# A two-block transformer kernel: the second layer's first norm in the last expert value steps, position tables from skewed rows, and the down projection's first halves in the gate loop

## The chip, the cores and the metric

One program runs on one core of a Trainium2 chip. The metric is the device time of one execution in microseconds (us). Engines: PE is TensorE (PEld its weight loads), DVE is VectorE, ACT is ScalarE, POOL is GpSimd, SP is SyncE, which issues the DMAs.

## The reference, cut to what matters

The program is one forward pass in float32 over 256 tokens and 256 context tokens, 1024 channels, in two blocks of two layers each. A layer of the first block is

```python
h = _modulate(_rmsnorm(x, norm1_g[l]), mod[0], mod[1])     # h * (1 + scale) + shift
p = h @ w_in[l]                                            # then four mixers, merged and added to x
h = _modulate(_rmsnorm(x, norm2_g[l]), mod[3], mod[4])
x = x + mod[5] * _peer(h, *peer_args)                      # 16384 experts, 16 of them for each of 8 heads
```

Context rows go through the same with their own modulation. `_peer` scores every expert against every token, and sums value rows with weights. A layer of the second block mixes (layer 0 a gated delta rule, layer 1 sparse attention with a relative position bias taken from `rel_bias`; both attend to a memory too), and then adds a gated feed-forward part:

```python
gate, val = jnp.split(h @ w_up, 2, axis=-1)
gate = causal_dwconv(gate, conv_w) + conv_b
return (jax.nn.silu(gate) * val) @ w_down                  # w_down is 2816 x 1024
```

## The kernel before, in words

Most products are made of three matmuls: each operand is split into a high half (ACT copies it to a rounded type) and a low half (DVE or POOL subtracts the high half), and high x high, high x low and low x high are summed in PSUM (`products_of`, L106). The program is a row of stages (`stage`, L53). Within a stage the engines run their own lists of instructions and meet by semaphores; at its end all of them wait for each other. K.ps is the eight PSUM banks of 128 x 512.

*Expert values.* `peer` (L1821) ends with U = 64 value steps for layer 0 (indices `m`; the DMA table of the page counts those of both layers as 128). Step m fetches 256 value rows (1 MB, `pr_w`), the kept scores (`pr_gs`) and the chosen weights (`pr_g`). DVE multiplies scores and weights (`multiply`, L2366), ACT and DVE split both operands (L2221, L2383 to L2394), and TensorE adds 6 products into each of 8 banks, two banks for each of four tiles of 128 tokens (`combine`, L2111): 48 matmuls a step. Step m's two operands must be split before it starts. SP waits for TensorE's step m before it refills that step's slot (L1945). After the last step, DVE adds the eight banks, times the modulation, to the rows x (L2396 to L2403).

*The second layer's first norm.* `first_norm` (L2507) is a stage of its own, and it calls `norm` (L499). SP fetches two small tables, a 480 KB table and the masks (`PositionsBeside`, L3594), four rows of modulation, the gain row and the first two weight tiles of the next projection. ACT squares four tiles of rows and takes the root; DVE makes (1 + scale) times gain, scales each tile and adds the shift; TensorE turns 32 blocks of 128 x 128; ACT copies the high halves, DVE subtracts for the low ones. Beside this TensorE makes the position tables: one product of 32 x 384 that is stored with a skew in DRAM (`po_rows`, for layer 1's bias), and 60 small ones for the bias of the compressed attention (`cmp_bias`). The next stage, `branch_inputs` (L2406), starts with the projection.

*Attention to memory.* `attend` (L3026) works through items: a score, its scaling and maximum on DVE, the exponential on ACT, two transposes, a copy on ACT, a product with the values and a scaling. Three items are under way at once. Layer 0 of the second block has 8 items. Before them SP fetches two tiles of the next projection's weights, 1.5 MB each; ACT splits the first behind the last item. `compressed_attention` (L3469) is the first stage of layer 1's attention.

*Feed-forward part.* `conv_glu` (L3688) runs J = 22 gate steps: TensorE makes gate and value columns, ACT copies the gate, DVE convolves, ACT takes silu, DVE multiplies and both split the result. SP fetches the first four tiles of `w_down` near the end. The next stage, `down` (L3798), splits a tile of `w_down` at each step k (ACT L3826, DVE L3853), and TensorE adds it into four banks in 12 matmuls; SP refills a slot when its low half is done, and at k = 8 it also fetches the gain row and, in layer 0, three 1 MB tiles of the next layer's projection, one behind the other. Its first matmul waits for the first low half.

## Time and profile before

| | |
|---|---|
| median of 3 runs | 4334.24 us (4333.1 to 4334.87) |
| profiled execution, its own time | 4332.16 us |
| span of the profile | 4330.4 us |
| mean granted clock of TensorE | 0.971 |
| PE / DVE / ACT / POOL busy | 94% / 62% / 43% / 10% of the span |
| DMA | 833 MB, 192 GB/s, q1 busy 57.4% of 16 engines |

Times in the rows are microseconds from the span's start. A timeline row gives start, duration, engine, line, operation, output<-inputs, shapes and count; in brackets stands how long the engine was idle before it and what ended that. Several operations of a kind in a row are merged (x8). A row of groups gives busy us and mean ns of one. The granted clock is 1.00 at 2.4 GHz and 0.50 at 1.2 GHz.

### The profile page before, as it was taken

What the parts mean: (1) busy time and instruction counts of PE and PEld (TensorE: products, weight loads), DVE (VectorE), ACT (ScalarE), POOL (GpSimd) and SP (SyncE); (2) the same over time, 40 slices, a digit from 0 to 9 for tenths busy, and PEclk for the clock granted to TensorE, in tenths of its full rate; (3) what the DMA queues carried; (4) which work ended last, traced back from release to release, by engine and by line L of the source; (5) the groups of instructions that cost most, each with busy time, mean ns of one, the idle gap of its engine ahead of it and who ended that gap; (6) DMA issues with size and microseconds to landing.
All of it is one profiled execution on the core that took longest, in us unless ns stands there. A gap on an engine that the chain in (4) does not pass through costs nothing. (4 is left out here: it accounts for less than half of the span.)

```text
span 4330.4 us, 62619 instructions
## 1 busy us (share of the span) xinstructions
PE 4084.7 (94%) x25222; PEld 3567.3 (82%) x25222; DVE 2704.3 (62%) x5412; ACT 1840.5 (43%) x2400; POOL 413.2 (10%) x118
## 2 busy tenths in 40 slices
PE   7999899999999999999989899999998988998898
PEld 5876788788877888888788799998886887988697
DVE  5736668899941455555575588754666664653665
ACT  3433233477743322222245445544444444543453
POOL 2222034200000000000004240000000012000000
PEclk8999999999999999999899999999999999999999
DMA  6431224377788777777544456777886522554354
GB/s 241 142 101 61 94 88 140 123 285 296 293 314 289 240 242 243 243 243 243 185 134 140 147 174 194 256 287 268 290 283 224 163 71 78 157 186 140 93 163 144
DMA packets 523642, 833.18 MB, mean 192 GB/s; under 512 B 20829, under 2 KB 398877, under 8 KB 502073
## 3 DMA queue, kind: packets, MB, share of 16 engines
q1 hardware_dynamic: 523354, 829.18, 57.4%
q8 instruction: 200, 3.28, 0.3%
q14 instruction: 88, 0.72, 0.1%
HBM read 692.19 MB, written 136.92 MB: 191 GB/s over the span
## 5 line engine op out<-in xcount | busy, mean ns | idle before, releaser
L113 PE MATMUL bank<-hThi_l,pr_whi 128*128 128x512 f32 (+1 forms) x2304 | 786.9, 342 | 16.6 <-DVE pr_wlo L2269 6.7
L113 PE MATMUL bank<-hTlo_l,pr_whi 128*128 128x512 f32 (+1 forms) x2304 | 779.1, 338 | 0.0
L113 PE MATMUL bank<-hThi_l,pr_wlo 128*128 128x512 f32 (+1 forms) x2304 | 777.6, 338 | 0.0
L113 PE MATMUL bank<-pr_whi,pr_ahi 128*128 128x512 f32 x1536 | 600.0, 391 | 9.7 <-DVE pr_alo L2393 9.7
L113 PE MATMUL bank<-pr_wlo,pr_ahi 128*128 128x512 f32 x1536 | 599.0, 390 | 0.0
L113 PE MATMUL bank<-pr_whi,pr_alo 128*128 128x512 f32 x1536 | 598.7, 390 | 0.0
L2151 ACT ACTIVATE pr_whi<-pr_w 128x2048 fp32r<-128x2048 f32 x270 | 517.2, 1915 | 126.7 <-DMA pr_w<-peer_v_in 124.0
L113 PEld LDWEIGHTS bank<-hThi_l,pr_whi 128*128 128x128 f32 x2304 | 441.1, 191 | 66.1 <-POOL pr_wlo L2026 8.1
L113 PEld LDWEIGHTS bank<-hThi_l,pr_wlo 128*128 128x128 f32 x2304 | 440.8, 191 | 46.1
L113 PEld LDWEIGHTS bank<-hTlo_l,pr_whi 128*128 128x128 f32 x2304 | 441.4, 192 | 42.2
L2269 DVE TENSOR_TENSOR pr_wlo<-pr_w,pr_whi 128x2048 fp32r<-128x2048 f32 x102 | 233.4, 2289 | 269.0 <-ACT pr_whi L2151 268.9
L113 PEld LDWEIGHTS bank<-pr_whi,pr_ahi 128*128 128x128 f32 x1536 | 289.0, 188 | 73.6 <-DVE pr_wlo L2386 11.1
L2221 ACT ACTIVATE pr_ahi<-pr_a 128x1024 fp32r<-128x1024 f32 (+1 forms) x128 | 108.5, 847 | 563.8 <-DVE pr_a L2377 364.5
L113 PEld LDWEIGHTS bank<-pr_whi,pr_alo 128*128 128x128 f32 x1536 | 289.2, 188 | 60.3
L113 PEld LDWEIGHTS bank<-pr_wlo,pr_ahi 128*128 128x128 f32 x1536 | 289.2, 188 | 59.6
L2165 ACT ACTIVATE pr_s<-bank 128x512 f32<-128x512 f32 (+1 forms) x256 | 125.2, 491 | 471.3 <-PE bank L113 454.2
L2386 DVE TENSOR_TENSOR pr_wlo<-pr_w,pr_whi 128x2048 fp32r<-128x2048 f32 x128 | 292.4, 2284 | 21.1 <-ACT pr_whi L2151 21.1
L1290 POOL TENSOR_TENSOR gr_wlo<-gr_w,gr_whi 128x2048 fp32r<-128x2048 f32 x30 | 137.4, 4580 | 1709.3 <-ACT gr_whi L1495 1709.3
L2375 DVE TENSOR_TENSOR pr_a<-pr_g 128x512 f32<-128x512 f32 x128 | 82.8, 689 | 307.9 <-DMA pr_g<-dense_weights 307.9
L2026 POOL TENSOR_TENSOR pr_wlo<-pr_w,pr_whi 128x2048 fp32r<-128x2048 f32 x40 | 188.3, 4708 | 379.0 <-ACT pr_whi L2151 379.0
L113 PE MATMUL bank<-gu_Thi,gu_whi 128*128 128x256 f32 x704 | 200.2, 284 | 3.5 <-PEq L61 3.5
L113 PE MATMUL bank<-hThi_l,gr_whi 128*128 128x512 f32 (+1 forms) x512 | 184.1, 360 | 17.0 <-ACT mx_gate L1578 7.3
(609 smaller groups left out, 8241.5 us busy)
## 6 DMA issues: line engine op xcount, KB each, us to landing
pr_w<-peer_u_in SPq DMA_DIRECT2D x128, 1024.0 KB, 5.7
pr_w<-peer_v_in SPq DMA_DIRECT2D x128, 1024.0 KB, 5.0
dense_weights<-pr_buf SPq DMA_DIRECT2D x20, 4096.0 KB, 16.4
pr_g<-dense_weights SPq DMA_DIRECT2D x64, 1024.0 KB, 9.1
gu_w<-ffn_w_up_in SPq DMA_DIRECT2D x88, 512.0 KB, 5.2
gr_w<-w_in_in SPq DMA_DIRECT2D x32, 1024.0 KB, 5.3
expert_scores<-pr_s SPq DMA_DIRECT2D x64, 512.0 KB, 7.1
pr_gs<-expert_scores SPq DMA_DIRECT2D x64, 512.0 KB, 5.9
```

What stands on the lines that cost most here:

```text
L113: ins = pe.matmul(psum, a, b, start=first and i == 0, stop=last and i == len(terms) - 1)
L1290: pool.tensor_tensor(w_lo[:, held.slot(n), :, :], wt[:, held.slot(n), :, :], w_hi[:, n % slots, :, :].bitcast(F32), ALU.subtract).then_inc ...
L2026: pool.tensor_tensor(w_lo[:, n % ring, :, :], wt[:, n % ring, :, :], w_hi[:, s, :, :].bitcast(F32), ALU.subtract).then_inc(lo_ready, 1)
L2151: act.activation(w_hi[:, n % slots, :, :], wt[:, n % ring, :, :], ACT.Copy).then_inc(hi_ready, 1)
L2165: act.activation(act_s[:, m % 3, j, :], K.ps[i % 4][:, 0:tw], ACT.Gelu_apprx_tanh).then_inc(freed, 1)
L2221: act.activation(a2[0][:, m % aslots, :, :], a[:, m % aslots, :, :], ACT.Copy).then_inc(a_hi, 1)
L2269: dve.tensor_tensor(w_lo[:, n % ring, :, :], wt[:, n % ring, :, :], w_hi[:, n % slots, :, :].bitcast(F32), ALU.subtract).then_inc(lo_later, 1)
L2375: last = dve.tensor_tensor(sums[:, :, e, :], both_halves[:, :, e, 0, :], both_halves[:, :, e, 1, :], ALU.add)
L2386: dve.tensor_tensor(w_lo[:, n % ring, :, :], wt[:, n % ring, :, :], w_hi[:, n % slots, :, :].bitcast(F32), ALU.subtract).then_inc(v_lo, 1)
```

## The change

Three things, in one edit.

1. The stage `first_norm` is gone. A class NextNorm is called from layer 0's `peer`. The last two value steps go by tiles of tokens: for each tile, both steps, then the next tile. When a tile's two banks are done, DVE adds them to x, ACT squares the tile and takes its root (a root per tile in place of one), DVE scales it in two halves, TensorE turns it (two tiles later), ACT copies the high half with the shift as a bias, and DVE makes the low half from the bank, the shift and the high half. The shift is now a column of 8 numbers per partition, and the copies and low halves are 128 wide (32 of each in place of 8 that were 512 wide). The scaled rows lie in slots of the value ring that are free by then. SP fetches modulation and gain at steps 10, 16 and 22, and the two weight tiles of the projection after the last multiply. (1 + scale) times gain is made at step 32 (`m == U // 2`).
2. The position tables' one product moves to the attention to memory of the second block's layer 0 (class Positions): the widening stands behind the first item's maximum on DVE, the product ahead of the first transposes on TensorE, the copy behind the first exponential on ACT, the store behind the weight tiles on SP. The 60 small products are gone: the compressed attention adds the masks to elements of the skewed bias instead (three small operations on DVE, ahead of the bias operation L3566).
3. In the last gate step ACT and DVE make both halves of the first two tiles of `w_down`; `down` starts with k = 2 on these engines, its slots are shifted by one, SP starts two fetches earlier without a wait, and the three next tiles are fetched at k = 9, 12 and 15.

`hT` and the projection's ring are allocated once for both layers.

```diff
+        if after:
+            spare = (first_v + U - 3) % 3
+            row_pairs = [wt[:, spare, :, :].rearrange("p (e j) c -> p e (j c)", e=2), held.wide[:, spare, :, :].rearrange("p (e j) c -> p e (j c)", e=2)]
+            after.hold(mem, lambda t: row_pairs[t // 2][:, t % 2, :])
...
+                    if after and m in (10, 16, 22):
+                        after.fetch(sp, (m - 10) // 6)
                 sp.wait_ge(mod_in, 32)
+                if after:
+                    sp.wait_ge(mulled, U)
+                    after.fetch_tiles(sp)
+                    after.land(sp)
...
+                for m in range(U - 2 if after else U):
+                    combine(m, range(outs))
+                for t in range(tiles if after else 0):
+                    for m in (U - 2, U - 1):
+                        combine(m, range(2 * t, 2 * t + 2), False)
+                    if t >= 2:
+                        after.turn(pe, t - 2)
+                for t in range(2 if after else 0):
+                    after.turn(pe, tiles - 2 + t)
...
+                for t in range(tiles if after else 0):
+                    if t >= 3:
+                        after.round_row(act, t - 3)
+                    after.square(act, t)
+                    after.root(act, t)
+                    if t == 0:
+                        after.first_hi(act)
+                for t in range(3 if after else 0):
+                    after.round_row(act, tiles - 3 + t)
...
+                    if after and m == U // 2:
+                        after.prepare(dve)
...
+                for t in range(tiles):
+                    if after and t:
+                        after.shift_square(dve, t - 1)
+                    add_out(2 * t)
+                    if after and t == 1:
+                        dve.wait_ge(used, U - 2)
+                    if after and t:
+                        after.scale_row(dve, t - 1)
+                    add_out(2 * t + 1)
+                    if after and t == 1:
+                        after.first_lo(dve)
+                if after:
+                    after.rest_of_row(dve, 0)
+                    after.shift_square(dve, tiles - 1)
+                    after.rest_of_row(dve, 1)
+                    after.scale_row(dve, tiles - 1)
+                    for t in range(2, tiles):
+                        after.rest_of_row(dve, t)
...
+class NextNorm:
...
+    def bank(self, g):
+        return self.K.ps[(6 + g) % 8][:, :].rearrange("f (n p) -> f n p", n=4)
+
+    def fetch(self, sp, i):
+        K, l = self.K, self.l
+        if i < 2:
+            sp.dma_start(self.scale[:, i, :], K.ada[l, i:i + 1, D:2 * D].broadcast_to([P, D])).then_inc(self.mods_in, 16)
+            sp.dma_start(self.shift[:, i, :], K.ada[l, i, 0:D].rearrange("(k p) -> p k", p=P), allow_slow_non_contiguous=True).then_inc(self.mods_in, 16)
+        else:
+            sp.dma_start(self.gain[:, :], K.dram["norm1_g"][l:l + 1, :].broadcast_to([P, D])).then_inc(self.mods_in, 16)
...
+    def prepare(self, dve):
+        dve.wait_ge(self.mods_in, 80)
+        for s in range(2):
+            dve.scalar_tensor_tensor(out=self.scale[:, s, :], in0=self.scale[:, s, :], scalar=1.0, in1=self.gain[:, :], op0=ALU.add, op1=ALU.mult).then_inc(self.step, 1)
+
+    def square(self, act, t):
+        if t:
+            act.wait_ge(self.squared, t)
+        act.wait_ge(self.done, 2 * t + 2)
+        act.activation(self.K.junk[:, 0:D], self.x[:, t, :], ACT.Square, scale=D ** -0.5, accum_out=self.ss[:, t:t + 1]).then_inc(self.squared, 1)
+
+    def root(self, act, t):
+        act.wait_ge(self.shifted, t + 1)
+        act.activation(self.ss[:, t:t + 1], self.ss[:, t:t + 1], ACT.Sqrt).then_inc(self.rooted, 1)
...
+    def scale_row(self, dve, t):
+        at = self.ss[:, t:t + 1]
+        dve.wait_ge(self.rooted, t + 1)
+        dve.reciprocal(at, at).then_inc(self.step, 1)
+        dve.wait_ge(self.step, t + 3)
+        for c in range(2):
+            part = slice(c * 512, (c + 1) * 512)
+            dve.scalar_tensor_tensor(out=self.h(t)[:, part], in0=self.x[:, t, part], scalar=at, in1=self.scale[:, t // 2, part],
+                                     op0=ALU.mult, op1=ALU.mult).then_inc(self.scaled, 1)
+
+    def turn(self, pe, t):
+        for g in range(2 * t, 2 * t + 2):
+            pe.wait_ge(self.scaled, g + 1)
+            for j in range(4):
+                k = 4 * (g % 2) + j
+                last = pe.transpose(self.bank(g)[:, j, :], self.h(t)[:, k * P:(k + 1) * P], self.K.ident[:, :])
+            last.then_inc(self.turned, 1)
+
+    def round_row(self, act, t):
+        for g in range(2 * t, 2 * t + 2):
+            at = self.place(g)
+            act.wait_ge(self.turned, g + 1)
+            for j in range(4):
+                k = at[0].start + j
+                last = act.activation(self.hT[0][:, k, at[1]], self.bank(g)[:, j, :], ACT.Identity, bias=self.shift[:, t // 2, k:k + 1])
+            last.then_inc(self.hi_done, 1)
+
+    def rest_of_row(self, dve, t):
+        for g in range(2 * t, 2 * t + 2):
+            at = self.place(g)
+            dve.wait_ge(self.hi_done, g + 1)
+            for j in range(4):
+                k = at[0].start + j
+                last = dve.scalar_tensor_tensor(out=self.hT[1][:, k, at[1]], in0=self.bank(g)[:, j, :], scalar=self.shift[:, t // 2, k:k + 1],
+                                                in1=self.hT[0][:, k, at[1]].bitcast(F32), op0=ALU.add, op1=ALU.subtract)
+            last.then_inc(self.lo_done, 1)
...
+class Positions:
...
+    def widen(self, dve):
+        dve.wait_ge(self.arrived, 32)
+        dve.tensor_copy(self.many[:, :, :], self.rel[:, :, None].broadcast_to([32, GH, P // GH])).then_inc(self.wide, 1)
+
+    def product(self, pe):
         pe.wait_ge(self.wide, 1)
+        pe.matmul(self.K.ps[7][:, 0:3 * P], self.many[:, :, :].rearrange("b h r -> b (h r)"), self.hot[:, :], start=True, stop=True).then_inc(self.spread, 1)
+
+    def take(self, act):
+        act.wait_ge(self.spread, 1)
+        act.activation(self.rows[:, :], self.K.ps[7][:, 0:3 * P], ACT.Copy).then_inc(self.rows_out, 1)
...
                 score(1)
+                if positions:
+                    positions.product(pe)
...
                 exponential(0)
+                if positions:
+                    positions.take(act)
...
                 maximum(0)
+                if positions:
+                    positions.widen(dve)
...
+                for t in range(2):
+                    seen = N_CMP if t else (P - 32) // 16 + 1
+                    at = 1 + (1 - t) * P // 16
+                    chain(dve.tensor_tensor(cmp_bias[:, t, :, 0:seen], bias[:, :, :].rearrange("p h (n i) -> p h n i", i=16)[:, :, at:at + seen, 15],
+                                      cm[:, 0, t, 0:seen][:, None, :].broadcast_to([P, GH, seen]), ALU.add))
+                    if seen < N_CMP:
+                        dve.tensor_copy(cmp_bias[:, t, :, seen:N_CMP], cm[:, 0, t, seen:N_CMP][:, None, :].broadcast_to([P, GH, N_CMP - seen]))
...
+                else:
+                    act.wait_ge(down_first, 32)
+                    for k in range(2):
+                        act.activation(buffers.down[0][:, k + 1, :], dn_w[:, k, :], ACT.Copy).then_inc(down_hi, 1)
...
+                if i == J - 1:
+                    for k in range(2):
+                        dve.wait_ge(down_hi, k + 1)
+                        dve.tensor_tensor(buffers.down[1][:, k + 1, :], dn_w[:, k, :], buffers.down[0][:, k + 1, :].bitcast(F32), ALU.subtract)
...
-                sp.wait_ge(lo_ready, k - 3)
+                if k >= 6:
+                    sp.wait_ge(lo_ready, k - 5)
                 sp.dma_start(w[:, k % 4, :], K.dram["ffn_w_down"][l][k * P:(k + 1) * P, :]).then_inc(loaded[k % 4], 16)
                 if k == 8:
                     sp.dma_start(behind.gain, behind.source).then_inc(gain_in, 16)
-                    if ahead:
-                        ahead.fetch(sp, first_in, rest_in)
+                if ahead and k in (9, 12, 15):
+                    ahead.fetch_tile(sp, (k - 9) // 3, first_in, rest_in)
...
-            for k in range(J):
+            for k in range(2, J):
...
-                act.activation(halves[0][:, k % 3, :], w[:, k % 4, :], ACT.Copy).then_inc(hi_ready, 1)
+                act.activation(halves[0][:, (k + 1) % 3, :], w[:, k % 4, :], ACT.Copy).then_inc(hi_ready, 1)
...
-                pe.wait_ge(lo_ready, k + 1)
+                if k >= 2:
+                    pe.wait_ge(lo_ready, k - 1)
...
```

## Rows read from the trace of the kernel before

**Rows 1.** Windows: five engines busy us (instructions), granted clock, DMA share, GB/s

```profile
1500.00:1600.00 100.00, 100.00 (x443) 82.84 (x442) 52.71 (x45) 26.72 (x18) 0.00 (x0) 1.00 0.80 252
...
2170.00:2175.00 5.00, 4.12 (x19) 4.15 (x20) 1.42 (x7) 1.91 (x1) 0.00 (x0) 0.50 0.23 36
```

**Rows 2.** Timeline of PE: start, duration, operation [idle before, releaser]

```profile
2134.20 0.39 PE L113 MATMUL bank<-pr_whi,pr_alo 128*128 128x512 f32 x1
...
2142.64 1.61 PE L3626 MATMUL bank<-po_hot,po_many 32*128 32x384 f32 x2 [8.06 <-DVE po_many L3635]
...
2144.05 12.80 PE L3630 MATMUL bank<-po_rel,po_chot 32*128 32x8 f32 x60
...
2170.88 0.55 PE L113 MATMUL bank<-hThi_l,wpair 128*128 128x256 f32 x1 [6.61 <-PEq L61]
```

**Rows 3.** Timeline of DVE around the old norm

```profile
2116.52 1.22 DVE L2393 TENSOR_TENSOR pr_alo<-pr_a,pr_ahi 128x1024 fp32r<-128x1024 f32 x1
...
2125.17 0.69 DVE L2400 TENSOR_TENSOR pr_tmp<-bank,pr_mod 128x512 f32<-128x512 f32 x1 [7.43 <-PE bank L113]
...
2126.51 0.69 DVE L2400 TENSOR_TENSOR pr_tmp<-bank,pr_mod 128x512 f32<-128x512 f32 x1
...
2149.76 2.36 DVE L2517 SCALAR_TENSOR_TENSOR mod_l<-mod_l,gain_l 128x1024 f32<-128x1024 f32 x2 [4.90 <-DMA gain_l<-norm_g_in]
...
2165.62 4.87 DVE L572 TENSOR_TENSOR hTlo_l<-bank,hThi_l 128x512 fp32r<-128x512 f32 x8
```

**Rows 4.** Timelines of ACT, DVE and PE at the end of layer 0's gate loop

```profile
3828.50 0.51 ACT L3735 ACTIVATE gu_cv<-gu_cv,gu_cb 128x256 f32<-128x256 f32 x1 [1.22 <-DVE gu_cv L3790]
...
3835.46 2.95 ACT L3826 ACTIVATE dn_hi<-gu_down_w 128x1024 fp32r<-128x1024 f32 x3 [0.81 <-PEq L61]
...
3831.25 0.35 DVE L3788 TENSOR_SCALAR gu_cv<-gu_gp,gu_cw 128x256 f32<-128x256 f32 x1 [1.45 <-ACT gu_gp L3749]
...
3834.67 0.42 DVE L3773 TENSOR_TENSOR gu_actlo<-gu_bs,gu_acthi 128x256 fp32r<-128x256 f32 x1
...
3837.82 0.50 PE L113 MATMUL bank<-dn_hi,gu_acthi 128*128 128x512 f32 x1 [4.15 <-DVE dn_lo L3853]
```

**Rows 5.** Waits in 3812 to 3910: who for whom, us, times, longest

```profile
ACT dn_hi L3826 <- DMA gu_down_w<-ffn_w_down_in: 7.4, 3, 7.0
...
PE bank L113 <- DVE dn_lo L3853: 6.3, 2, 4.2
```

**Rows 6.** Groups by form: busy us, mean ns | idle before

```profile
L3141 DVE SCALAR_TENSOR_TENSOR b_cat<-bank,at_weight,b_cat 128x128 f32<-128x128 f32 x32 | 11.2, 351 | 8.2 <-PE bank L3075 7.6
...
L642 DVE SCALAR_TENSOR_TENSOR xrows<-xrows,small,dn_gain 128x512 f32<-128x512 f32 x4 | 2.7, 746 | 0.0
...
L3106 ACT ACTIVATE at_pt<-bank 128x128 f32<-128x128 f32 x16 | 4.1, 256 | 0.0
...
L3095 ACT ACTIVATE at_pr<-at_sc,at_max 128x128 f32<-128x128 f32 x16 | 6.4, 401 | 3.5 <-DVE at_max L3128 3.4
```

**Rows 7.** Timeline of ACT in the old norm

```profile
2136.39 1.06 ACT L533 ACTIVATE junk<-xrows 128x1024 f32<-128x1024 f32 x1 [20.89 <-PEq L61]
...
2141.10 1.28 ACT L535 ACT_TABLE_LOAD   x1
```

**Rows 8.** Groups of 1500 to 2100, the expert value loop of layer 0

```profile
L2375 DVE TENSOR_TENSOR pr_a<-pr_g 128x512 f32<-128x512 f32 x110 | 71.1, 689 | 273.4 <-DMA pr_g<-dense_weights 273.4
```

**Rows 9.** DMA issues of 2170 to 2174: KB, median us to landing

```profile
bi_wb<-cv_dw_b_in SPq DMA_DIRECT2D x1, 1.0 KB, 1.8
```

**Rows 10.** DMA issues of 2136 to 2170

```profile
po_hot<-bucket_rev_in SPq DMA_DIRECT2D x1, 48.0 KB, 2.2
```

**Rows 11.** Timeline of PE in layer 0's attention to memory

```profile
3640.69 0.69 PE L3066 MATMUL bank<-ident,at_pr 128*128 128x128 f32 x2 [0.75 <-ACT at_pr L3095]
```

**Rows 12.** Timeline of DVE in the compressed attention

```profile
3995.22 0.19 DVE L3568 COPY nc_kcT<-bank 128x30 f32<-128x30 f32 x1 [7.84 <-PE bank L3522]
```

**Rows 13.** Windows by stretch, the start of layer 0's down projection

```profile
3838.00:3843.00 5.00, 5.00 (x16) 3.91 (x17) 2.04 (x2) 0.94 (x2) 0.00 (x0) 0.66 0.78 238
```

More of the change, by code:

```diff
@@ L462, in fetch, with fetch_tile @@
                 sp.dma_start(dst, src).then_inc(rest if i else first, 16)
+    def fetch_tile(self, sp, i, first, rest):
+        for dst, src in self.tiles[i]:
+            sp.dma_start(dst, src).then_inc(rest if i else first, 16)
     def land(self, sp, first, rest):
@@ L496, in ahead, with norm @@
         return Ahead(tiles, self.halves[0][:, 0, :, 0:cw], self.halves[1][:, 0, :, 0:cw], self.wt[:, 0, :, 0:cw])
-def norm(K, rows, tiles, gain_of, shift_of, out, chans=None, loads=(), prepare=None, ahead=None, beside=None):
+def norm(K, rows, tiles, gain_of, shift_of, out, chans=None, loads=(), ahead=None):
     n = len(tiles)
@@ L503, in norm @@
     groups = [(i, c) for i in range(n) for c in range(0, KD, 4)] if chans is not None else []
-    with stage(K, "squared", "eps_added", "rooted", "step", "scaled", "turned", "hi_done", "lo_done", "loads_in", "first_in", "rest_in", "ahead_hi",
-               *(beside.names if beside else ())) as \
-            (block, squared, eps_added, rooted, step, scaled, turned, hi_done, lo_done, loads_in, first_in, rest_in, ahead_hi, *others):
-        if beside:
-            beside.use(*others)
+    with stage(K, "squared", "eps_added", "rooted", "step", "scaled", "turned", "hi_done", "lo_done", "loads_in", "first_in", "rest_in", "ahead_hi") as \
+            (block, squared, eps_added, rooted, step, scaled, turned, hi_done, lo_done, loads_in, first_in, rest_in, ahead_hi):
         def bank(g):
@@ L1814, in __init__ @@
         self.lo = mem.enter_context(K.nc.sbuf_tensor(f"pr_wlo{l}", [P, ring, KD, 256], F32R))
+        with K.nc.sbuf_tensor(f"pr_wide{l}", [P, self.slots, KD, 256], F32) as wide:
+            self.wide = wide
         self.hi = mem.enter_context(K.nc.sbuf_tensor(f"pr_whi{l}", [P, self.slots, KD, 256], F32R))
@@ L2119, in combine @@
                     pe.wait_ge(a_lo, m + 1)
-                    for o in range(outs):
+                    for o in wanted:
                         t, c = divmod(o, 2)
@@ L2523, in first_layer, with branch_ring @@
+def branch_ring(K, l):
+    with ExitStack() as upper:
+        upper.enter_context(K.nc.sbuf_tensor(f"ring_hole_l{l}", [P, 67 * 256], F32))
+        ring = Ring(K, upper, KD, MIX + 16, 2)
+        side = ModulationBeside(K, l, upper) if l == 0 else None
+    return ring, side, ring.ahead(K.dram["w_in"][l], [(CV_OFF, MIX), (CV_OFF + MIX, MIX)])
+def first_layer(K, l, x, s_cols, hT, hT_wide, rings):
     nc = K.nc
@@ L3023, in _, with attend @@
                 close(1, a, four(o[:, 1], a))
-def attend(K, items, scale, ahead):
+def attend(K, items, scale, ahead, positions=None):
     nc = K.nc
@@ L3625, in tensor @@
+    def product(self, pe):
         pe.wait_ge(self.wide, 1)
-        pe.matmul(K.ps[6][:, 0:3 * P], self.many[:, :, :].rearrange("b h r -> b (h r)"), self.hot[:, :], start=True, stop=True).then_inc(self.spread, 1)
-        for t in range(2):
-            for n in range(N_CMP):
-                c = (t * N_CMP + n) * GH
-                last = pe.matmul(K.ps[7][:, c:c + GH], self.chot[:, t, n, :], self.rel[:, :], start=True, stop=True)
-        last.then_inc(self.spread, 1)
-    def first(self, dve):
-        dve.wait_ge(self.arrived, 64)
-        dve.tensor_copy(self.many[:, :, :], self.rel[:, :, None].broadcast_to([32, GH, P // GH])).then_inc(self.wide, 1)
-        dve.wait_ge(self.spread, 1)
-        dve.tensor_copy(self.rows[:, :], self.K.ps[6][:, 0:3 * P]).then_inc(self.rows_out, 1)
@@ L3935, in build @@
         s_cols = K.s_cols = sb("s_cols", [P, KD, 2])
-        cmp_bias = sb("cmp_bias", [P, 2, GH, N_CMP])
-        for l in range(DEPTH):
-            first_layer(K, l, x, s_cols, cmp_bias)
+        with ExitStack() as first:
+            hT_hi = first.enter_context(nc.sbuf_tensor("hThi", [P, KD, TALL], F32R))
+            with nc.sbuf_tensor("hTwide", [P, KD, TALL], F32) as hT_wide:
+                pass
+            hT = hT_hi, first.enter_context(nc.sbuf_tensor("hTlo", [P, KD, TALL], F32R))
+            rings = [branch_ring(K, l) for l in range(DEPTH)]
+            for l in range(DEPTH):
+                first_layer(K, l, x, s_cols, hT, hT_wide, rings)
         x2 = x[:, 2:4, :]
         K.tri, K.mem = sb("tri", [P, P]), mem
-        second_block(K, x, cmp_bias)
+        second_block(K, x)
 def buckets(dist):
```

185 lines of the change are left out of this document (86 added, 99 removed).

## The prediction

> **What bounds the kernel now.** I read the page first: TensorE is busy 94% of the span, so time is lost only where TensorE stands still or works on something small. The windows by stretch then show one large hole, between the expert values of layer 0 and the first projection of layer 1. When TensorE comes out of it, the granted clock is 0.50, the lower of its two levels (1.2 GHz), for the first 5 us of the projection [rows 1]. TensorE's own order of time gives its edges: the last value matmul starts at 2134.20 (0.39 long), the first projection matmul at 2170.88 [rows 2]. That is 36.3 us in which TensorE does 60 tiny table products (12.8 us) and 32 transposes. The same view of VectorE shows why the hole lasts: its norm waits for the gain row until 2149.76 and its last low half ends at 2165.62 + 4.87 = 2170.49; 0.39 us later the next stage begins [rows 2, 3]. Two further holes are at the end of the gate loops (TensorE starts the down projection at 3837.82 after 4.15 us idle, and likewise in the other layer) and one is inside layer 0's down projection (6.3 - 4.15 = 2.15 us, behind a 7.0 us wait for weights) [rows 4, 5].
>
> **Part 1, the norm: what bounds it after the change.** I take the trace's times and lay the new order over them. A value matmul starts every 0.227 us (443 of them fill 100 us [rows 1]; 48 a step: the two last steps run from 2112.8 to 2134.6). Now rows of tokens go one after the other, each with 24 matmuls, 5.44 us.
> - TensorE, row 0: twelve matmuls of step 62 until 2115.5. Then step 63, the last, is wanted, whose low half ends at 2116.52 + 1.22 = 2117.74 [rows 3]; before, it was wanted only at 2123.7. A new stall of 2.2 us. Rows 0 to 3 then end at 2120.5, 2126.0, 2131.4 and, with 8 transposes between (0.9 us), 2137.8.
> - VectorE: adding half a row takes 1.34 us (two starts of L2400 [rows 3]), so 2.7 a row. Scaling a row is two 512-wide operations of 0.746 [rows 6], 1.4 + 0.2 for the reciprocal. The first low half of the projection's weights, moved as it is, takes 2.3. The new low halves are 128 wide with a pointer, as L3141, 0.351 us each [rows 6]; back to back they overlap by some 0.07, so 8 take 2.2 us, against 1.2 for the two 512-wide ones that they replace.
> - ScalarE: a square is 1.06 + 0.19 us, the root's table is loaded once, 1.28 [rows 7]. The high halves are 128-wide copies, now with a bias from a pointer. The plain copy is 0.256, the 128-wide exponential with a bias pointer 0.401 [rows 6]. I take 0.39, 0.30 back to back, 2.4 us a row: it is nearest to the form that has the pointer.
> - Laid end to end: row 0 is added by 2122.1 and squared by 2123.3; root 2124.8 (table). Row 1 is added by 2129.2, the weights' low half done 2131.4. Row 2 added by 2135.9, its root 2137.6. Row 3 added by 2141.7, squared 2142.9. VectorE meanwhile makes row 0's low half, 2141.7 to 2143.8, and adds eps to row 3 (2143.9); root 2144.1. ScalarE can round row 1 only after that root, to 2146.6; VectorE's low half of row 1 ends 2147.7, row 3 is scaled by 2149.4, row 2's low half ends 2151.5, row 3's 2153.7. With 0.39 for the stage and half a microsecond for the chance that the clock falls in the new stall, the projection starts at 2154.6 instead of 2170.9: **16.3 us gained**.
> - Bounds: with the plain copy's 0.256 and low halves at the 0.28 of a plain 128-wide operation, 13 such on the path, the end is near 2151.5 (19 us gained). With every semaphore hop of some 0.25 us missed at a dozen handovers, and the clock falling in the new stall (1.7 us on TensorE), it is near 2158 (13 us).
>
> The Trainium skill, page "ScalarE: Activation LUTs", section "What ACT_TABLE_LOAD costs", gives a pointer operand some 93 ns more per ACTIVATE, here against the change: 32 copies with a pointer in place of 8 wide ones. The traced 0.401 with a pointer against 0.256 without agrees in sign. By that page's 280 + 0.833 x 128 = 387 ns my end stands; without its rule it would be some 1 us earlier.
>
> What is moved in front costs nothing as I read it. In the value loop VectorE waits 273.4 us over 55 steps for the weighted choices, 5.0 a step [rows 8], and another 6.0 us lie between its last low half and TensorE's need. So the two 1.2 us scale operations at step 32 vanish, and so do two 512 KB rows, two column loads and one gain row on SP's queue at steps 10, 16 and 22: if a column load holds the queue 4 us (1024 packets of 4 bytes; 256 such landed in 1.8 us [rows 9]), the next weights land 4 us later and are still in time. If that cover were gone, each would cost its own length. The weights of the projection (2 MB) are fetched after the last multiply, 2114.4, and have 10 us until ScalarE wants the first. The projection itself starts at half clock as before: nothing gained.
>
> **Part 2, tables from skewed rows.** The 60 products and the table's arithmetic go with the old stage, counted above. The product that spreads the rows comes back in layer 0's attention to memory, and there it is on the path. The two loads start with the stage (3637.9), the second lands 2.2 us after its issue [rows 10], 3640.5; VectorE widens to 3640.7; TensorE's product is 1.61 us [rows 2], to 3642.35, and the first transposes, which stood at 3640.69 [rows 11], come 1.7 us late. ScalarE's copy of 384 columns (0.5) stands ahead of the second exponential: 2.1 late. All eight items follow, and so does the end of the stage: **2.0 us lost**. Bounds: 0.5 if later items catch up, 3.5 if the 1.5 MB store, behind 3 MB of output weights, ends the stage. The three small operations in the compressed attention stand ahead of 7.84 us in which VectorE waits for TensorE [rows 12]: nothing, and at most 1.0 if that cover were gone.
>
> **Part 3, down projection.** Two copies (2 x 1.06) go ahead of ScalarE's silu at 3828.50, of which 1.2 us were idle: silu 0.9 late. Two low halves (2 x 1.22) go on VectorE ahead of the last convolution, which stood at 3831.25: they run 3830.3 to 3832.7, after them a 0.4 low half, so it starts at 3833.0. Of the 1.75 us, 0.5 is absorbed, since the last product waited for TensorE anyway: the stage ends 1.2 later than 3834.67 + 0.42 = 3835.1. In return the down stage's first matmul no longer waits for 1.06 + 1.22: TensorE starts 0.4 after the stage does, 3836.7, not 3837.82 [rows 4]. Gain 1.1, twice: 2.2. The clock fell in the gap of 4.15 us (0.66 over the 5 us behind it [rows 13]) and I expect it to fall in one of 3.1 us as well; bounds 0 and 5.5 for both layers, the upper if neither falls. In layer 0 the three 1 MB tiles no longer go into the queue together: each takes some 2.8 us of it, and a weight has 4.6 us of slack at 2.8 us a step. The stall of 2.15 us [rows 5] goes; bounds 1 and 2.5. **4.3 us gained**.
>
> **Sum.** 16.3 - 2.0 + 4.3 = 18.6 us off the profiled 4332.16 is 4313.6. The median of the runs is 2.1 us above the profiled run, so I forecast 4334.24 - 18.6 = **4315.6 us**. Part 1 alone moves every later stage against the clock's changes; that moves single microseconds either way.
>
> **Rivals.**
> - The tail is bound by handovers between three engines, not by VectorE's sum, and the two other parts bring nothing: 13 - 3.5 + 1 = 10.5 gained, 4323.7. For: row 3 passes through eight handovers. Against: in my schedule VectorE hardly idles after 2124. 12%.
> - The clock is kept in the gaps before the down projections, and the tail is at its lower bound: 19 - 1.5 + 6.5 = 24, 4310. Against: the gaps shrink by a quarter only, and the clock fell in the old ones [rows 13]. 10%.
> - ScalarE's tables: if square, root and identity did not share a set, each of four rows would load twice, 8 x 1.28 = 10 us, 5 to 8 of it on the path: 4322. Against: after the one load of the old root and in the down stage, squares and root follow with one load (here [rows 7]). 5%.
> - The change doesn't do what it says: the new stall becomes the bound because fetches of steps 62 and 63 come later. They are issued as before, so 3%, 4326.
> - The slower side: the column loads starve TensorE. They stand on SP's queue ahead of the next weighted choices. With 5.0 + 6.0 us of slack, of which I trust 6, it takes over 15 us a load for two of them to eat 18.6 us; at 25 us each, 2 x 19 - 18.6 = 19 slower, 4354. For: 4-byte packets, 1024 a load. Against: 256 of them took 1.8 us. 5%.
>
> **How the numbers follow.** Forecast 65%, the rivals as above. A measurement of this kernel can tell 0.2%, 8.7 us, from no change. Faster by more than that: the forecast, the first rival mostly, the second and third: 0.90. Within: 0.05. Slower: 0.05. Range: the bounds of the three parts, not all at one end, and so that both first rivals are inside: 4309 to 4324.
>
> **What would show it.** Right: a stall of about 2.2 us on TensorE before the second half of row 0; the first projection matmul some 20 us after the last value matmul would have ended (2154 to 2156); one table load there; VectorE busy over 90% from 2131 on; 2 us more between first and second transposes in layer 0's attention; no wait for weights in layer 0's down projection. Wrong: any TensorE gap in the value loop at steps 10 to 23, or more than one table load in the tail.

## The result, and the profile after

| | before | after |
|---|---|---|
| median of the runs beside each other | 4333.67 us | 4298.1 us |
| ratio after to before, 95% interval | | 0.9929, 0.9916 to 0.9943 |
| the same comparison, repeated with 5 runs and 16 | 4327.73 us | 4297.15 us, 0.9934, 0.9921 to 0.9948 |
| profiled execution, its own time | 4332.16 us | 4297.31 us |
| span, mean granted clock | 4330.4 us, 0.971 | 4295.5 us, 0.972 |
| PE / DVE / ACT / POOL busy | 94 / 62 / 43 / 10% | 95 / 63 / 43 / 10% |

By the ratios the change gains 29 to 31 us (0.0066 and 0.0071 of 4330); the medians lie 30.6 and 35.6 us apart. I had forecast 18.6 and a range that ended at 4309: the kernel is faster than that.

First the timeline of TensorE around the norm, then of ScalarE and VectorE there.

```profile
2116.14 0.48 PE L113 MATMUL bank<-pr_whi,pr_ahi 128*128 128x512 f32 x1 [2.33 <-DVE pr_alo L2407]
...
2139.89 0.66 PE L2630 MATMUL bank<-ident,pr_wide 128*128 128x128 f32 x4
2147.66 1.97 PE L2630 MATMUL bank<-ident,pr_wide 128*128 128x128 f32 x8 [7.11 <-DVE pr_wide L2622]
2152.80 0.55 PE L113 MATMUL bank<-hThi,wpair 128*128 128x256 f32 x1 [3.17 <-PEq L61]
```
```profile
2123.37 1.28 ACT L2602 ACT_TABLE_LOAD   x1
...
2137.25 2.17 ACT L2639 ACTIVATE hThi<-bank,nn_shift 128x128 fp32r<-128x128 f32 x8
...
2141.08 2.15 DVE L2648 SCALAR_TENSOR_TENSOR hTlo<-bank,nn_shift,hThi 128x128 fp32r<-128x128 f32 x8
...
2144.59 2.16 DVE L2648 SCALAR_TENSOR_TENSOR hTlo<-bank,nn_shift,hThi 128x128 fp32r<-128x128 f32 x8 [1.30 <-ACT hThi L2639]
```

The new stall is there (2.33 us, foretold 2.2), one table load, and the projection starts at 2152.80. The after trace runs 1.74 us ahead before the changed place, so [rows 2]'s 2170.88 stands for 2169.14: 16.3 us gained.

The start of either down projection (TensorE, layer 0 and 1), and three of ScalarE's copies in layer 1, first after, then before. These copies wait for TensorE, so their distance is the length of one step of 12 matmuls.

```profile
3816.56 1.19 PE L113 MATMUL bank<-dn_pair,gu_acthi 128*128 128x512 f32 x2 [2.56 <-PEq L61]
...
4226.89 0.70 PE L113 MATMUL bank<-dn_pair,gu_acthi 128*128 128x512 f32 x2 [2.57 <-PEq L61]
...
4238.13 1.06 ACT L3974 ACTIVATE dn_pair<-gu_down_w 128x1024 fp32r<-128x1024 f32 x1 [1.66 <-PE bank L113]
4240.85 1.06 ACT L3974 ACTIVATE dn_pair<-gu_down_w 128x1024 fp32r<-128x1024 f32 x1 [1.66 <-PE bank L113]
4243.57 1.06 ACT L3974 ACTIVATE dn_pair<-gu_down_w 128x1024 fp32r<-128x1024 f32 x1 [1.66 <-PE bank L113]
```
```profile
4258.42 0.80 PE L113 MATMUL bank<-dn_hi,gu_acthi 128*128 128x512 f32 x1 [4.15 <-DVE dn_lo L3853]
...
4271.54 1.06 ACT L3826 ACTIVATE dn_hi<-gu_down_w 128x1024 fp32r<-128x1024 f32 x1 [1.73 <-PE bank L113]
4274.34 1.06 ACT L3826 ACTIVATE dn_hi<-gu_down_w 128x1024 fp32r<-128x1024 f32 x1 [1.74 <-PE bank L113]
4277.14 1.06 ACT L3826 ACTIVATE dn_hi<-gu_down_w 128x1024 fp32r<-128x1024 f32 x1 [1.74 <-PE bank L113]
```

The gap of [rows 4], 4.15 us, is 2.56. And a step takes 2.72 us, not 2.80: the same 12 matmuls with all operands long in place, at full clock. That is 0.227 and 0.233 us a matmul. 22 steps in two layers make 3.5 us that no step of my sum held.

The attention to memory of layer 0 (TensorE):

```profile
3615.91 2.04 PE L3198 MATMUL bank<-ma_kT,b_qmT 128*128 128x256 f32 x4 [9.48 <-PEq L61]
3618.33 1.64 PE L3781 MATMUL bank<-po_hot,po_many 32*128 32x384 f32 x2 [0.37 <-DVE po_many L3777]
3619.91 0.69 PE L3205 MATMUL bank<-ident,at_pr 128*128 128x128 f32 x2
```

The first transposes come 4.00 us after the first score, before 3640.69 - 3637.89 = 2.80 [rows 11]: 1.2 later; the stage is 1.3 longer (19.2 us from its first score to the transposes of the next stage, before 17.9).

### The profile page after: what moved, and what is told of

Same layout as the page of the kernel before. It is cut to its first block and busy times, and to the rows that moved or that the text cites. A ratio compares the mean times of both kernels' runs of the same rounds, so it can differ in the third digit from the quotient of the medians.

```text
span 4295.5 us, 62547 instructions
## 1 busy us (share of the span) xinstructions
PE 4066.1 (95%) x25162; PEld 3553.6 (83%) x25162; DVE 2703.1 (63%) x5442; ACT 1844.2 (43%) x2428; POOL 412.4 (10%) x118
## 5 line engine op out<-in xcount | busy, mean ns | idle before, releaser
L113 PE MATMUL bank<-hThi,pr_whi 128*128 128x512 f32 (+1 forms) x2304 | 787.0, 342 | 17.5 <-DVE pr_wlo L2283 7.3
L113 PE MATMUL bank<-hTlo,pr_whi 128*128 128x512 f32 (+1 forms) x2304 | 779.0, 338 | 0.0
L113 PE MATMUL bank<-hThi,pr_wlo 128*128 128x512 f32 (+1 forms) x2304 | 778.0, 338 | 0.0
L113 PEld LDWEIGHTS bank<-hThi,pr_whi 128*128 128x128 f32 x2304 | 441.5, 192 | 67.2 <-POOL pr_wlo L2024 8.4
L113 PEld LDWEIGHTS bank<-hThi,pr_wlo 128*128 128x128 f32 x2304 | 440.7, 191 | 45.7
L113 PEld LDWEIGHTS bank<-hTlo,pr_whi 128*128 128x128 f32 x2304 | 441.7, 192 | 42.2
L113 PE MATMUL bank<-hThi,gr_whi 128*128 128x512 f32 (+1 forms) x512 | 184.6, 361 | 19.5 <-ACT mx_gate L1562 10.1
```

The source lines that it names most:

```text
L113: ins = pe.matmul(psum, a, b, start=first and i == 0, stop=last and i == len(terms) - 1)
```

## The experiments

**First: where are the other 10 us?** Theory A: the down projection part is worth more than 4.3 us, the rest is chance of the clock. Theory B: once the norm ends earlier, every later stage meets the clock's changes at better places, each time.

*after_again*: no edit.

> The changed kernel once more, unaltered, to narrow its gain and to see what a second profiled run of the same kernel does in stretches that the change doesn't touch. Theory A (the three parts gain about 24 us: norm 16.3, down projections some 9 instead of 4.3, tables -1.3; the rest of the difference of the two traces is clock changes that fall elsewhere by chance): ratio 0.9935 to 0.9950, and the stretches outside the three parts differ by single microseconds between the two profiled runs of this kernel. Theory B (moving the later stages systematically saves another 6 to 10 us at TensorE's clock): ratio again 0.9925 to 0.9932, and the untouched stretches repeat their times to within 1 us.

Measured: 4297.15 us, ratio 0.9934 (0.9921 to 0.9948). From the end of TensorE's 4.2 us gap behind layer 1's mixers to the 9.5 us gap ahead of the attention to memory nothing is changed. This stretch took 1168.7 us in the first profiled run of this kernel and 1161.9 in the second (before: 1168.8). So identical code differs by 7 us from run to run, as much as theory B wanted to explain. The ratio falls between the ranges of the two theories and decides nothing.

*wait_back*, behind the last low half of the norm:

```
+ for i in range(13):
+     chain(dve.tensor_tensor(tmp[:, :, :]..., mod5[:, 0, :], mod5[:, 1, :], ALU.mult))
```

> The changed kernel with 13 unneeded multiplications of 128x1024 on VectorE behind its last low half of the norm, some 16.3 us, so that layer 1's projection starts as late as before the change; all else as after. Theory A: the kernel becomes slower by the wait alone, 16 us, and the later stretches take what they take in the changed kernel, give or take 3 us. Theory B (the gain of the norm is multiplied later by the clock): 22 to 26 us slower than the changed kernel.

```profile
2155.72 16.33 DVE L2443 TENSOR_TENSOR pr_tmp<-pr_mod 128x1024 f32<-128x1024 f32 x13
...
2172.66 0.55 PE L113 MATMUL bank<-hThi,wpair 128*128 128x256 f32 x1 [19.63 <-PEq L61]
```

Measured: 4314.15 us, ratio 0.9967 (0.9955 to 0.9979), 17.0 us over after_again for 16.33 us of filling (14 by the ratios, some 8 us either way). Theory B wanted 22 to 26, at or beyond the end of that interval: nothing here asks for more than the norm's own stage shows.

*down_undone*: the classes and functions `GluBuffers`, `conv_glu` and `down` as they were before, all else as after (so the allocation line, too, is the old one). *down_only*: the reverse.

> The changed kernel with the down projection part taken back (its first two halves made in the down stage, the three tiles of the next projection fetched together at step 8), norm and tables as changed. The prediction's term: 4.3 us slower than the changed kernel. Theory A: 8 to 10 us slower, layer 0 from the end of the gate loop to the end of the down projection 4.8 us longer and layer 1 4.3 us longer, because the clock falls in both gaps before the down projection. Rival (chance of the clock): each layer 2 to 3 us longer, the rest elsewhere.

> The kernel before with the down projection part alone. The prediction's term: 4.3 us faster than before. Theory A: 8 to 10 us faster. Both: TensorE's gap ahead of either down projection 2.6 us and not 4.15, no wait for weights in layer 0's down projection; nothing changes before the gate loop's last step of layer 0.

Measured: down_undone 4311.08 us, ratio 0.9963 (0.9949 to 0.9977), 13.9 us slower than after_again. down_only 4316.33 us, ratio 0.9974 (0.9963 to 0.9985), 11.4 us faster than before. From TensorE's last gate matmul to its last down matmul, down_undone takes 69.4 and (to the end of the span) 77.0 us, after 64.2 and 71.2: 11.0. The traces say 11 us and the times agree within their intervals, where I had 4.3 and theory A 8 to 10. The down part is where my sum was short. down_undone is also Part 1 and Part 2 alone: it is 16.0 us faster than before by its ratio, where the two parts measure 16.3 - 1.3 = 15.0 in the traces.

**Second: what makes a step 2.72 us?** The diff also lays the two halves of a row side by side (`dn_pair`) and begins them elsewhere (a hole of 21464 elements, before 20464).

*pair_only* is before with `dn_pair` after the old hole of 20464; *apart* is after with `dn_hi` and `dn_lo` after the new hole of 21464; *pair_low* is after with `[P, 21464]` made `[P, 20464]`; *fetch_only* is down_undone with the tiles spaced (`if ahead and k in (9, 12, 15)`).

> The kernel before with one line of the allocation altered: the high and the low half of a down projection row stand side by side in one buffer (3 slots of 2 x 4 KB) instead of in two buffers 12 KB apart, and the buffer begins where the high halves began (20464). Nothing moves in time otherwise. In the traces so far a step of the down projection (12 matmuls) takes 2.80 us where the halves stand apart and 2.72 where they are a pair. Theory distance (what counts is how far apart the two halves of one row stand): 2.72 a step, 22 steps twice, 3.5 us faster in all. Theory address (what counts is where the buffer begins, 21464 against 20464): 2.80 a step, no change. Theory order (the halves made one step earlier, other fetches beside): 2.80, no change.

> The changed kernel with the high and low halves of the down projection in two buffers again, 12 KB apart, the first beginning at the changed place (21464); the order of work stays as changed. Distance: 2.80 us a step, 3.5 us slower than the changed kernel. Address: 2.72, no change. Order: 2.72, no change. All: the gaps ahead of the down projections stay 2.6 us.

> The changed kernel with the pair beginning at 20464, where the high halves began before. Distance: 2.72 us a step. Address: 2.80. Order: 2.72. With the two others of this call it tells the three theories apart.

> The changed kernel without the early halves and without the pair; of the down projection part only the spacing is kept: the three 1 MB tiles of the next projection are fetched at steps 9, 12 and 15 and not together at 8. If the stall at step 8 is the fetch's: the 1.0 us longer step 8 of layer 0 that the kernel without the part shows (3.82 against 2.80) goes, all else as there (gaps 4.15 us, 2.80 us a step, half clock behind both gaps), so 1 to 2 us faster than it and some 11 slower than the changed kernel. If the stall comes from the late start of the halves: it stays.

ScalarE's copies in layer 1, of pair_only, of apart, and of pair_low:

```profile
4263.52 1.06 ACT L3825 ACTIVATE dn_pair<-gu_down_w 128x1024 fp32r<-128x1024 f32 x1 [1.74 <-PE bank L113]
4266.32 1.06 ACT L3825 ACTIVATE dn_pair<-gu_down_w 128x1024 fp32r<-128x1024 f32 x1 [1.74 <-PE bank L113]
```
```profile
4240.84 1.06 ACT L3975 ACTIVATE dn_hi<-gu_down_w 128x1024 fp32r<-128x1024 f32 x1 [1.66 <-PE bank L113]
4243.56 1.06 ACT L3975 ACTIVATE dn_hi<-gu_down_w 128x1024 fp32r<-128x1024 f32 x1 [1.66 <-PE bank L113]
```
```profile
4251.62 1.06 ACT L3974 ACTIVATE dn_pair<-gu_down_w 128x1024 fp32r<-128x1024 f32 x1 [1.74 <-PE bank L113]
4254.42 1.06 ACT L3974 ACTIVATE dn_pair<-gu_down_w 128x1024 fp32r<-128x1024 f32 x1 [1.74 <-PE bank L113]
```

The steps take 2.80, 2.72 and 2.80 us. With the pair at the old address the step stays slow, in the old order and in the new one; without the pair at the new address it is fast: the address counts, the pairing does not, and the new order alone does not bring it (whether it is needed, the fifth part tells). pair_only 4329.87 us (0.9993, 0.9985 to 1.0002), apart 4295.72 (0.9918), pair_low 4306.07 (0.994). fetch_only: 4309.65 us, 0.9947 (0.9932 to 0.9961), the stall of layer 0 is gone, as is its row among the waits (down_undone, layer 0):

```profile
ACT dn_hi L3966 <- DMA gu_down_w<-ffn_w_down_in: 6.2, 3, 5.7
```

So the stall was the fetch's. By the times fetch_only can't be told from down_undone.

**Third: what about the address?** A matmul has a loaded operand (128x128) and a streamed one (512 or 256 columns wide). The allocations lie one behind the other, so each operand's first byte can be worked out, and with it how far the loaded operand begins behind the streamed one. (Sizes are taken as rounded up to 32 bytes; only so do the gate loop, which lies behind buffers of odd sizes, and the experts, which don't, give the same offsets for the same rates.) I first took this offset modulo 128.

*shift_mixed*, *shift_64* and *shift_gates* are after with holes changed (elements of 4 bytes; layer 0, layer 1):

```
                  dn_hole  hole_a (gate weights)  pr_shift (layer 1 experts)  gr_hole
shift_mixed       20472    408 + (8, 24)[l]       8                           16384
shift_64          21464    408 + 16               16                          16384
shift_gates       21448    408                    24                          16384 + 16
```

> The changed kernel with buffers moved by a few bytes and nothing else. In all traces so far a 512-wide matmul starts every 227 ns where the two operands begin at the same offset modulo 128 bytes and every 233 where they are 32 or 64 bytes off. Here the pair of the down projection begins 4000 - 32 bytes lower than in the changed kernel (hole 20472), again 0 modulo 128 against the activations. Theory offset: 2.72 us a step (at hole 20464, 32 bytes lower, it was 2.80). Theory region: 2.80. Beside it the gate loop's weights are moved by 32 bytes in layer 0 and 96 in layer 1, and the expert ring of layer 1 by 32: theory offset says that 256-wide matmuls leave 120 ns for about 115 there, 10 us less over both gate loops and up to 17 us less in layer 1's experts; theory region says 120 stays.

> The changed kernel with the gate loop's weights (both layers) and the expert ring of layer 1 moved by 64 bytes, so that their matmuls, 256 wide, find the two operands 64 bytes off modulo 128. Theory offset: 120 ns become 113 to 118; 2112 matmuls of the gate loops and some 3350 of the experts at 2 to 7 ns each, 11 to 37 us faster than the changed kernel. Theory region: no change, within 2 us.

> The changed kernel with the merge gates' ring moved by 64 bytes, so that its operands now begin at the same offset modulo 128. Theory offset: the 512-wide gate matmuls of layer 0 go from 233 to 227 ns (735 of them, 4.7 us less), the 256-wide ones of layer 1 from 115 to 120 (some 700, 3 us more). Beside it the down projection's pair is moved 64 bytes lower: 2.80 us a step if 64 off is as bad as 32, 2.72 if only 32 is bad; and layer 1's expert ring by 96 bytes, to see whether 96 off does what 32 does.

Windows of TensorE alone (busy us (matmuls), granted clock, DMA share, GB/s), in layer 1's gate loop: after, then shift_64.

```profile
4100.00:4140.00 40.00, 40.00 (x336) 1.00 0.64 177
```
```profile
4100.00:4150.00 50.00, 50.00 (x444) 1.00 0.65 192
```

40 us hold 336 matmuls, one every 0.119 us; 50 us hold 444, one every 0.113. The same in layer 1's experts (all five engines), after, then shift_64:

```profile
2700.00:2800.00 100.00, 100.00 (x851) 100.00 (x850) 78.38 (x222) 49.80 (x67) 0.00 (x0) 1.00 0.66 227
```
```profile
2700.00:2800.00 100.00, 100.00 (x874) 100.00 (x873) 81.52 (x235) 50.29 (x69) 0.00 (x0) 1.00 0.67 232
```

shift_64: 4279.41 us, ratio 0.9888 (0.987 to 0.9906), some 18 to 20 us under the changed kernel (0.9934 there) for 64 bytes. By the traces both gate loops took 125.7 and 125.3 us instead of 132.6 and 132.9 and layer 1's experts with their values 736.1 instead of 755.3, 33 us in all; the times, 4268 to 4286, show about half to two thirds of that. Some of it went where the faster loop now waits, a gap of 3.21 us ahead of the down projection instead of 2.56; behind it the clock fell in both layers, and the two down projections took 2.9 us more. The rest I can't place. shift_mixed 4293.82 (0.9916), shift_gates 4300.84 (0.9932). But shift_mixed's step took 2.79 us at 0 modulo 128, and shift_gates' gates 232.8 ns: for the 512-wide matmuls the rule modulo 128 fell. At offsets of 32 and 96 bytes the 256-wide ones took 117 to 118 ns, where I had expected about 115.

**Fourth: the period, and a kernel that uses it.** *pair_256* is after with a dn_hole of 21400 and a gr_hole of 16384 + (112, 0)[l]. *best* is shift_64 with gr_hole 16384 + (48, 64)[l], the hole ahead of the output projection's ring 14272 + 16, and

```
- if t >= 3: after.round_row(act, t - 3)     # ScalarE, ahead of the square of row t
+ if t >= 2: after.round_row(act, t - 2)
+ if t == 2: after.rest_of_row(dve, 0, (0,)) # VectorE; rows' low halves split in two groups
...
- both low halves of w_down ahead of the last convolution
+ one ahead of it, one behind it
```

> The changed kernel with the down projection's pair 256 bytes lower (hole 21400) and the merge gates' ring of layer 0 moved by 448 bytes, to 768 off its other operand: both offsets are now odd multiples of 256. Theory period 256: 2.72 us a step and 227 ns for the gates. Theory period 512: 2.80 and 233. Theory region (the pair must end where the activations begin): 2.80, and the gates stay at 233.

> The kernel shift_64 with more of the same: the gate ring of layer 0 at 512 bytes off (227 ns instead of 233 if the period is 256 or 512, 4.7 us; 233 by theory region), that of layer 1 at 576 (64 modulo 512), the output projection's weights 64 bytes higher (some 530 matmuls from 120 to 113 ns, 3.5 us). In the norm ScalarE makes the high halves of row 0 ahead of the square of row 2 and those of row 1 ahead of row 3's, and VectorE fills its two waits of 1.3 us with low halves: the projection 2.3 us earlier. In the gate loop one of the two early low halves goes behind the last convolution: 0.5 us earlier, twice. Together 11 us faster than shift_64; 3 if only the norm and the gate loop do what they should.

> The kernel shift_64 once more beside best, for the comparison on one chip. By its first run 0.4% faster than the changed kernel; by the rates of its trace (2112 matmuls 6.7 ns faster, 3340 at 5.2 ns) 31 us, 0.7%. Here 4266 to 4280 us.

pair_256: 2.72 us a step and 227.8 ns in the gates, 4294.52 us (0.9923). So the period is 256 bytes, and an offset of 0 is where the 512-wide matmul is fast. best: **4261.77 us, ratio 0.9855 (0.9838 to 0.9871)**, with shift_64_again 4279.27 (0.9889) beside it: 17.5 us less, where I expected 11. Its norm, TensorE:

```profile
2141.05 1.97 PE L2635 MATMUL bank<-ident,pr_wide 128*128 128x128 f32 x8 [4.70 <-DVE pr_wide L2627]
2146.19 0.55 PE L113 MATMUL bank<-hThi,wpair 128*128 128x256 f32 x1 [3.17 <-PEq L61]
```

The wait for the last scaled row is 4.70 us, not 7.11: 2.4 gained. Its gates run at 227.9 ns, and its window from 300 to 400 holds 432 matmuls (before 422). Its gaps ahead of the down projections are 2.54 us, and the clock was kept behind both. The output projection's matmuls went from 120.0 to 117.8 ns only, not to 113: here the weights are the streamed operand, so 64 bytes up puts the loaded one at -64, which is 192 modulo 256, and not at 64.

**Fifth: the address without the change.** *before_down_offset* is before with `[P, 20464]` made `[P, 20504]`; *before_offsets* adds the 16 elements of shift_64 at its two places.

> The kernel before with one number altered: the hole ahead of the down projection's halves is 20504 elements and not 20464 (160 bytes more), which puts them at 0 modulo 256 against the activations. Theory offset: 2.72 us a step in place of 2.80, in both layers, 3.5 us faster by the trace (less than the interval of the times can tell); the gaps of 4.15 us and the stall of layer 0 stay. Any theory by which the changed order is needed for it: 2.80.

> The same, and the gate loop's weights and layer 1's expert ring 64 bytes off, as in shift_64: 256-wide matmuls at 113 to 115 ns instead of 120. By the rates 3.5 + 14 + 17 = 35 us faster than before, the order of work being that of the kernel before; by the times of shift_64 (18 us under the changed kernel) about 22. Rival: without the changed gate loop end, the last step of the faster gate loop waits longer for VectorE and each gap ahead of the down projection grows by 1 us: 33 and 20.

ScalarE's copies in before_down_offset:

```profile
4273.11 1.06 ACT L3826 ACTIVATE dn_hi<-gu_down_w 128x1024 fp32r<-128x1024 f32 x1 [1.66 <-PE bank L113]
4275.83 1.06 ACT L3826 ACTIVATE dn_hi<-gu_down_w 128x1024 fp32r<-128x1024 f32 x1 [1.66 <-PE bank L113]
```

2.72 us from one number. The time doesn't show it: 4327.1 us, 0.9997 (0.9987 to 1.0006). Layer 1's down projection takes 61.75 us instead of 63.42. Layer 0's takes 66.4 and not 65.8: the steps behind the 1 MB fetches take 5.69, 4.00 and 3.22 us, and the clock fell in that stall. The fall is not the offset's doing: in pair_only, at 2.80 us a step, the clock fell there too (5.26, 4.17, 3.07), and in before_offsets, at 2.72, it didn't (5.69, 2.85). What the shorter steps lose is the longer wait, 5.69 against 5.09 in before: 0.6 us. So in layer 0 the offset pays fully only where the fetches are spaced too. before_offsets: 4300.3 us, 0.9944 (0.9931 to 0.9958): 24 to 27 us with no instruction altered, nearly what the whole change brings and between my two expectations. The rival is out: both gaps stayed at 4.15 us.

## Why the prediction was wrong

| term | foretold | between the two traces |
|---|---|---|
| norm (Part 1) | 16.3 | 16.3 |
| tables (Part 2) | -2.0 | -1.3 |
| start of both down projections | 2.2 | 3.2 (4.15 - 2.56, twice) |
| stall of layer 0 | 2.15 | 2.4 (steps of 5.09 and 2.91 instead of 2.80) |
| clock kept in layer 1 | 0 | 1.6 (first step 4.45, now 2.82) |
| rate of the down matmuls | not in the sum | 3.5 |
| sum | 18.6 | 25.7 |

**Part 1** held to the tenth at its end, which is in part luck. Stall, one load and low halves of 2.15 us per row came as foretold. But the rows were added 1 to 2 us later than in my schedule (row 0 by 2123.9, not 2122.1, on the clock of the trace before), since VectorE waited for TensorE and ScalarE: it was busy 88% from 2131 on, where I had written over 90%. ScalarE needed 2.17 us a row and not 2.4, and the half microsecond that I had added for the clock made up the rest. One copy with the pointer measures 397 ns (mean of 32), as the Trainium skill, page "ScalarE: Activation LUTs", section "What ACT_TABLE_LOAD costs", would have it (387, an estimate by its 280 ns and 0.833 ns a column). Back to back, one starts every 0.25 us. What I had not seen is that VectorE waited 1.28 and 1.30 us for ScalarE, which did squares and roots ahead of copies that were due; *best* took that back. wait_back shows no sign that the norm's gain is eaten or multiplied later.

**Part 2** was right in place and 0.7 too dear: the loads land sooner, the product starts 0.37 us behind the last score and the first transposes come 1.2 us late, not 1.7. The three small operations of the compressed attention cost nothing that the trace shows: from TensorE's 4.8 us gap there to its 3.8 us gap it is 17.3 us with them and 17.0 to 17.3 without, in every trace but that of before itself (20.5, of which 17.1 at the low clock and not 10.5 as elsewhere). No experiment separates this part; its 1.3 us are read from the traces alone, but the attention stage is 1.3 to 1.6 us longer in all of those with the change than in all of those without.

**Part 3** is the step that failed, 4.3 us against 10.7 in the traces and 11.4 and 13.9 in the times. The causes that it named were right, and the stall was the fetches' (fetch_only). The gap shrank by 1.6 and not 1.1: the last convolution came 1.3 us late and not 1.75, since the silu ahead of it was 0.6 late and not 0.9, so the stage ended 0.75 us later and not 1.2. Behind a gap of 4.15 us the first step took 4.4 to 5.3 us, 3.3 us of it or more at the low clock, all 12 times. Behind one of 2.56 it took 4.3 to 4.4 in layer 0 in 7 of 9 traces and in layer 1 in 1 of 9 (2.8 to 2.9 otherwise), so my "fall in one of 3.1 us as well" held for one layer. In the other layer the same code fell in one trace and not in eight, so that term is in part chance. My range left that out, too: it ended at 25 us gained, while my own bounds for the three parts, the clock kept in both layers among them, add up to 19 - 0.5 + 10.2 = 28.7. And the largest miss, 3.5 us that the sum put at nothing, is the allocation line of the diff: I took the rate of the down matmuls as given. I read the line as bookkeeping for the halves' earlier life; it moved the streamed operand, and the loaded one now begins 0 and not 160 bytes modulo 256 behind it. The profile of before held the sign: 2.80 us a step here against 12 x 0.227 = 2.72 in the value loop [rows 1], for the same matmul.

**The rest**, 29 to 31 less 25.7, is within the intervals (some 5 us each), and most of it has a place that my sum doesn't have. From layer 1's first projection matmul to the end of TensorE's 4.2 us gap behind its mixers it is 287.3 to 288.7 us in the five traces with the old norm and 284.4 to 285.3 in twelve of the thirteen with the new one (288.2 in shift_gates, which slows the gates there): some 3 us. wait_back has them too, so they don't come from the stage's earlier time; down_only doesn't, so they aren't Part 3's. Part of it is a wait for the mixers' weights and the clock behind it (TensorE, before, then after):

```profile
2419.48 6.67 PE L1337 MATMUL bank<-zTs_l,mx_wb 128*128 128x256 f32 x16 [4.54 <-DMA mx_wb<-w_branch_in]
```
```profile
2399.83 5.36 PE L1321 MATMUL bank<-zTs_l,mx_wb 128*128 128x256 f32 x16 [3.77 <-DMA mx_wb<-w_branch_in]
```

Which line of the change does it, no run tells. That the two profiled runs differ by 34.9 is chance in part: 1.7 us lie ahead of the changed place, 3.1 are the compressed attention of before (20.5 us, above), and the unchanged stretch named above took from 1161.9 to 1172.2 us over twelve traces. The rival "clock kept, tail at its bound" (4310) had half of its cause right; column loads, table reloads and starving fetches did not occur.

## What to carry to other kernels

Before a sum is closed, divide each long matmul loop's time by its count and compare with the fastest loop of the same shape: a few ns per matmul can be an address (here 6.5 of 233), and a hole of 64 bytes is a cheap edit to try. Read an allocation line in a diff as a change of speed until its offsets are worked out. Where one engine waits a microsecond for another in a tail, look at what that other does first out of turn.

## What the runs showed of the hardware

The start-to-start distance of matmuls at full clock (loaded operand 128x128, both in the rounded fp32 type) by the offset of the two operands' first bytes modulo 256, means over the matmuls of a trace whose start times follow without a gap (some 500 to 3300 of them). Down is the down projection, gates are the merge gates of the first block, experts the query and expert scores (layer 0 512 wide, layer 1 256 wide):

| offset | 512 wide | 256 wide |
|---|---|---|
| 0 | 226.8 down, 227.3 experts, 227.8 gates | 120.0 gate loop, 119.9 experts |
| 32 | | 118.3, 118.4 |
| 64 | 233.3 down, 233.3 gates | 113.3 gate loop, 114.7 experts, 115.2 gates |
| 96 | | 117.3, 117.8 |
| 128 | 232.4 down, 232.8 gates | 118.8 gates |
| 160 | 233.4 down | |
| 192 | | 117.8 output projection |

The two widths want opposite things: 64 bytes cost 6.5 ns at 512 columns and gain 6.7 at 256. It is the distance of the two operands that counts and not where they lie: in the gate loop both begin at 0 modulo 256 in before and both at 64 in after, at 120.0 ns each time. Why, the runs don't tell. Whether experts and gates miss the 113.3 of the gate loop by their 512-column row stride was not tried.
